# A two-layer streaming encoder step: the hand-over from the input projection to attention, norm and table factors in PSUM, and the places of eight output products

## What is computed

```python
# layer 0
h = rmsnorm(x, norm_mix[0])
q, k, v, u, g = split(h @ w_in)                     # u, g through gelu; 8 heads of 64
att = stick_breaking(q, k, v)                       # prompt: causal; sample: 512 cached rows + 64 new
sg  = u * (tril(w_s) @ g + b_s)                     # spatial gating in chunks of 128
x  += concat(att, sg) @ w_out
x  += swiglu(rmsnorm(x, norm_ffn[0]))               # hidden width 2816
# layer 1
h = rmsnorm(x, norm_mix[1])
s = scan(a * s + B h);  y = C s + d * h             # complex diagonal SSM, 64 groups of 64 states
x += glu(gelu(y) @ w_glu)
x += swiglu(rmsnorm(x, norm_ffn[1]))
y = rmsnorm(x, norm_final)
```

## Time and profile before

| | |
|---|---|
| median of 3 runs | 2650.52 us (2648.42 to 2651.08) |
| the profiled execution | 2645.23 us, its span 2643.1 us |
| busy share of the span | PE 95%, PEld 85%, DVE 46%, ACT 35%, POOL 50% |
| mean granted clock of PE | 0.972 of full speed |
| transfers | 322 MB, mean 122 GB/s |

### The profile page before, as it was taken

One profiled execution on the slowest core, in us unless ns is written; L12 is line 12 of the kernel. 1 busy time (PEld: TensorE's weight loads), 2 busy tenths in 40 slices (PEclk: granted clock), 3 DMA queues, 4 the chain that ended last, 5 costly groups with the idle time before them and its releaser, 6 DMA issues.

```text
span 2643.1 us, 39417 instructions
## 1 busy us (share of the span) xinstructions
PE 2506.9 (95%) x15914; PEld 2257.7 (85%) x15914; DVE 1221.8 (46%) x2074; ACT 926.2 (35%) x1334; POOL 1315.8 (50%) x840
## 2 busy tenths in 40 slices
PE   8999658899999989999999998999999999999998
PEld 6999646677778978899999987788887988999998
DVE  5896937765562242434343414544354133233233
ACT  5323237566552232312222323322224234221213
POOL 5465344655555554634343556544445556444444
PEclk9999879899999999999999999999999999999999
DMA  6227564334424555344444332445553222322221
GB/s 196 74 88 272 193 181 106 91 113 121 114 73 145 159 154 161 109 130 131 126 138 121 105 97 78 149 136 150 155 153 113 80 77 88 101 84 88 77 84 68
DMA packets 413731, 322.45 MB, mean 122 GB/s; under 512 B 86561, under 2 KB 370145, under 8 KB 412401
## 3 DMA queue, kind: packets, MB, share of 16 engines
q1 hardware_dynamic: 406464, 292.07, 37.5%
q0 software_dynamic: 5936, 26.69, 2.5%
q10 hardware_dynamic: 1152, 1.18, 0.1%
HBM read 258.78 MB, written 61.10 MB: 121 GB/s over the span
## 4 chain that ended last, share of the span: by engine, by line
PE 82%; DVE 8%; POOL 4%; DMA 3%; issue 2%; ACT 1%; SPq 0%; POOLq 0%; DVEq 0%; ACTq 0%
PE ps L256 24%; PE ps L257 23%; PE ps L258 23%; PE ps L752 3%; PE ps L764 2%; PE ps L1605 1%; PE ps L1601 1%; POOL wlo L250 1%; DMA mst<-mT 1%; DVE t L2071 1%; PE ps L744 1%; PE ps L740 1%; PE ps L1582 1%; DVE t L2073 1%; DVE nf L1351 1%
## 5 line engine op out<-in xcount | busy, mean ns | idle before, releaser
L250 POOL TENSOR_TENSOR wlo<-raw,whi 128x1024 fp32r<-128x1024 f32 x332 | 803.0, 2423 | 678.0 <-ACT whi L246 676.7
L256 PE MATMUL ps<-hB,whi 128*128 128x320 f32 (+1 forms) x1792 | 534.2, 298 | 3.4 <-POOL lB L1772 3.2
L246 ACT ACTIVATE whi<-raw 128x1024 fp32r<-128x1024 f32 x332 | 346.3, 1052 | 544.6 <-PE ps L258 403.7
L257 PE MATMUL ps<-lB,whi 128*128 128x320 f32 (+1 forms) x1792 | 531.2, 296 | 0.0
L258 PE MATMUL ps<-hB,wlo 128*128 128x320 f32 (+1 forms) x1792 | 531.2, 296 | 0.0
L1282 DVE TENSOR_TENSOR fb<-ps,ab 128x512 f32<-128x512 f32 (+2 forms) x156 | 83.5, 535 | 813.2 <-PE ps L258 722.9
L256 PE MATMUL ps<-rh,whi 128*128 128x512 f32 (+2 forms) x1056 | 356.5, 338 | 35.2 <-POOL rl L1252 21.9
L256 PE MATMUL ps<-hA,whi 128*128 128x512 f32 x896 | 358.3, 400 | 12.6 <-POOL lA L1240 12.3
L257 PE MATMUL ps<-lA,whi 128*128 128x512 f32 x896 | 351.7, 392 | 0.0
L258 PE MATMUL ps<-hA,wlo 128*128 128x512 f32 x896 | 351.4, 392 | 0.0
L257 PE MATMUL ps<-rl,whi 128*128 128x512 f32 (+2 forms) x1056 | 349.2, 331 | 0.0
(11 more groups left out here) (308 smaller groups left out, 3897.8 us busy)
## 6 DMA issues: line engine op xcount, KB each, us to landing
raw<-in_ffn_w_gate SPq DMA_DIRECT2D x88, 512.0 KB, 3.9
raw<-in_ffn_w_up SPq DMA_DIRECT2D x88, 512.0 KB, 3.8
raw<-in_ffn_w_down SPq DMA_DIRECT2D x88, 512.0 KB, 3.3
raw<-in_ssm_w_glu SPq DMA_DIRECT2D x32, 512.0 KB, 4.0
raw<-in_ab_w_in SPq DMA_DIRECT2D x20, 512.0 KB, 3.9
raw<-in_ab_w_out SPq DMA_DIRECT2D x16, 512.0 KB, 3.9
bt<-dBT SPq DMA_DIRECT2D x16, 512.0 KB, 5.1
tm<-dT SPq DMA_DIRECT2D x16, 512.0 KB, 4.2
```

The source lines that it names most:

```text
L246: act.activation(whi[:, slot(t), :], raw[:, t % 2, :], ACT.Copy).then_inc(sem("w_hi"), 1)
L250: pool.tensor_tensor(wlo[:, slot(t), :], raw[:, t % 2, :], whi[:, slot(t), :].bitcast(F32), ALU.subtract).then_inc(sem("w_lo"), 1)
L256: pe.matmul(out, wh, rh, start=first, stop=False)
L257: pe.matmul(out, wh, rl, start=False, stop=False)
```

## The change

Four parts: the SSM factors move to PSUM and their stores to earlier places; the loads of the hand-over are reordered and its conditions split in two; norm factors move to PSUM; six `outS` products go beside every second step.

```diff
-        g4, _ = plan(off_end + T * 4, ("g4", [P, 2, GP, 4], F32))
+        g4 = ps[:, 3, 256:512].rearrange("p (r j k) -> p r j k", r=2, k=4)
+        pbs = ps[:, 3, 0:2 * 8 * L].rearrange("p (r j k) -> p r j k", r=2, k=L)
+        pcs = ps[:, 3, 256:256 + 2 * 8 * (L + 1)].rearrange("p (r j k) -> p r j k", r=2, k=L + 1)
...
-        msum, mrm, oa = plan(off_w + 10 * D * 4, ("msum", [P, 2, 512], F32), ("mrm", [P, 2, 512], F32))
+        msum, mrm, oa = plan(off_w + 10 * D * 4, ("msum", [P, 2, 512], F32), ("mrm", [P, 512], F32))
+        ms3, oa = plan(off_w + 10 * D * 4 + 3 * 512 * 4, ("ms3", [P, 512], F32))
...
+        def products_done(eng):
+            eng.wait_ge(sem("acc_ready"), NC * IN_TILES)
+            eng.wait_ge(sem("z_lo"), 8)
+            eng.wait_ge(sem("mix_sent0"), 16 * 6)
+            eng.wait_ge(sem("mix_sent1"), 16 * 6)
...
-        new_slot([group("outS", 0, 0, m, [ts[m // 2]]) for m in range(4)])
-        for m in range(4, 8):
+        new_slot([group("outS", 0, 0, m, [ts[m // 2]]) for m in range(2)])
+        for m in range(2, 8):
+            new_slot(at=some_steps())
             new_slot([group("outS", 0, 0, m, [ts[m // 2]])], at=some_steps())
...
+        def mst_at(i):
+            return {2: nsq[:, 1, :], 3: ms3}.get(i, mst[:, i % 2, :])
         def mst_in(sp, i):
-            if i >= 2:
+            if i >= 4:
                 sp.wait_ge(sem("ms_lo"), i - 1)
+            if i == 2:
+                sp.wait_ge(sem("tables"), 18)
...
         def mid_sp(sp, ahead):
-            front_done(sp)
+            products_done(sp)
+            for i in range(4):
+                mst_in(sp, i)
+            sp.wait_ge(sem("tok_out0"), tok_sent(14))
             v_early(sp, 0)
             kq_early(sp, 1)
-            mst_in(sp, 0)
-            mst_in(sp, 1)
             x_load(sp, 0)
+            front_done(sp)
             v_early(sp, 1)
-            mst_in(sp, 2)
-            mst_in(sp, 3)
...
         def mid_act(act):
-            front_done(act)
+            products_done(act)
-            for S in SLOTS:
+            for no, S in enumerate(SLOTS):
+                if no == FIRST_DENSE:
+                    front_done(act)
...
         def mid_pe(pe):
-            pe.wait_ge(sem("kv_used"), kv_taken(len(TOKS)))
++                if no == FIRST_DENSE:
+                    pe.wait_ge(sem("kv_used"), kv_taken(len(TOKS)))
...
-                        if q >= 2:
-                            act.wait_ge(sem("m_f"), KD * (q - 1))
-                        act.activation(mrm[:, q % 2, 0:n], ps[:, G[g]["bank"], 0:n], ACT.Sqrt, bias=epsb[:, 0:1], scale=1.0 / D
+                        factor_free(act, q)
+                        act.activation(factor(q), ps[:, G[g]["bank"], 0:n], ACT.Sqrt, bias=epsb[:, 0:1], scale=1.0 / D
...
+        def factor(q):
+            k, half, c = NORMS[q]
+            n = HCH[half][c][1]
+            return mrm[:, 0:n] if q in (0, 2) else ps[:, 4 if c else 7, 0:n]
+        def factor_free(act, q):
+            if q == 1:
+                act.wait_ge(sem("o_out"), sum(v["last"] for v in units) - GROUPS_A)
+            elif q:
+                act.wait_ge(sem("m_f"), KD * (q if NORMS[q][2] == 0 else q - 1))
+            k, half, c = NORMS[q]
+            if k == 3 or q == 6:
+                act.wait_ge(sem("s_sh"), KD * (2 if k == 3 and half else 1))
...
-                p_ = [pb[:, r, j0:j0 + 8, :].unsqueeze(3).to_broadcast(sh) for r in range(2)]
+                own(dve.tensor_copy(pbs, pb[:, :, j0:j0 + 8, :]))
+                p_ = [pbs[:, r].unsqueeze(3).to_broadcast(sh) for r in range(2)]
...
-        PREP_AT = [12, 13, 14, 14, 15, 15, 16, 16, 17, 18, 19, 19]
+        PREP_AT = [(9, 0), (10, 0), (11, 0), (11, 1), (12, 1), (13, 0), (13, 1), (14, 0), (14, 1), (15, 0), (16, 0), (17, 0)]
...
+                if t == IN_TILES + 2:
+                    xg_free(sp)
+                    kq_first(sp)
                 if t - 4 in TOK_AT:
                     tok_store(sp, TOK_AT.index(t - 4))
-                if t == IN_TILES + 2:
-                    xg_free(sp)
-                    kq_first(sp)
```

More of the change, by code:

```diff
@@ L1028, in build @@
         NG = len(G)
+        FIRST_DENSE = G[0]["slot"]
         NSLAB = IN_TILES + len(SRC)
@@ L1097, in mst_in @@
                     sp.wait_ge(sem(f"o_stored{b}"), 16 * 4)
-            sp.dma_start(mst[:, i % 2, 0:n], mT[tile * P:(tile + 1) * P, s:s + n]).then_inc(sem(f"ms_in{i % 2}"), 16)
+            sp.dma_start(mst_at(i)[:, 0:n], mT[tile * P:(tile + 1) * P, s:s + n]).then_inc(sem(f"ms_in{i if i < 4 else i % 2}"), 16)
         def mst_cut(i):
@@ L1102, in mst_cut @@
             n = HALF[half][1]
-            return half, slice(tile * n, (tile + 1) * n), mst[:, i % 2, 0:n]
+            return half, slice(tile * n, (tile + 1) * n), mst_at(i)[:, 0:n]
         xs3 = xs.rearrange("p (f t) -> p f t", f=KD)
@@ L1166, in mid_act @@
                     half, cs, src = mst_cut(i)
-                    act.wait_ge(sem(f"ms_in{i % 2}"), 16 * (i // 2 + 1))
+                    act.wait_ge(sem(f"ms_in{i if i < 4 else i % 2}"), 16 if i < 4 else 16 * (i // 2))
                     if i == 4:
@@ L1231, in mid_pool @@
         def mid_pool(pool):
-            front_done(pool)
+            products_done(pool)
             pre_zero(pool)
-            for S in SLOTS:
+            for no, S in enumerate(SLOTS):
+                if no == FIRST_DENSE:
+                    front_done(pool)
                 for t in S["slabs"]:
@@ L1296, in mid_dve @@
         def mid_dve(dve):
-            front_done(dve)
-            for S in SLOTS:
+            products_done(dve)
+            for no, S in enumerate(SLOTS):
+                if no == FIRST_DENSE:
+                    front_done(dve)
                 gs, at = S["groups"], S["at"]
@@ L1331, in mid_dve @@
                         used(dve, rms_of[q])
-                        dve.reciprocal(mrm[:, q % 2, 0:n], mrm[:, q % 2, 0:n]).then_inc(sem("m_rr"), 1)
+                        dve.reciprocal(factor(q), factor(q)).then_inc(sem("m_rr"), 1)
                         dve.wait_ge(sem("m_rr"), q + 1)
-                    xf, rf = xh[half][:, cols_of(half, f, s, n)], mrm[:, q % 2, 0:n]
+                    xf, rf = xh[half][:, cols_of(half, f, s, n)], factor(q)
                     if q in SPLIT_NO:
@@ L2101, in prep_dve_block @@
                 sh = [P, 8, L + 1, 16]
-                p_ = [pc[:, r, j0:j0 + 8, :].unsqueeze(3).to_broadcast(sh) for r in range(2)]
+                own(dve.tensor_copy(pcs, pc[:, :, j0:j0 + 8, :]))
+                p_ = [pcs[:, r].unsqueeze(3).to_broadcast(sh) for r in range(2)]
                 c_ = [ct[:, r, j0:j0 + 8, :].unsqueeze(2).to_broadcast(sh) for r in range(2)]
@@ L2199, in store, with prep_stores @@
                 pool.dma_start(lo[j * P:(j + 1) * P, :], zlo[:].bitcast(F32)).then_inc(sem("z_stored"), 16)
+            def prep_stores(t, late):
+                for n in range(12):
+                    if PREP_AT[n] == (t, late):
+                        prep_pool_block(pool, n)
             for t in range(IN_TILES):
                 slab_lo(pool, t + 2)
-                for n in range(12):
-                    if PREP_AT[n] == t:
-                        prep_pool_block(pool, n)
+                prep_stores(t, 0)
                 if 2 <= t <= 8 and t % 2 == 0:
@@ L2214, in _ @@
                     cache_pool(pool, TOK_AT.index(t))
+                prep_stores(t, 1)
             at_pool_make(pool)
```

## The result

The changed kernel takes 2605.66 us (median of four runs, 2602.91 to 2605.96), the kernel before 2649.85 us: a ratio of 0.983, 95% interval 0.981 to 0.985, 44.2 us less.

The account below looks back on a forecast made before the run. TensorE's fixed-order queue was taken as the bound, time being won where it idles or its clock is low. Front 41, norms 10 and a slab split 1 made 52 us: 2650.5 - 52 = 2598 us, range 2584 to 2618.

Parts of the forecast that it names:

- Tables: VectorE's SSM tables: end at 297 us instead of 326; 20 us of waiting and 21 of holding go, 10 given back.
- My lower bound of 282 us: Earliest end forecast for VectorE's SSM tables, if no operation is held by GpSimd.
- GpSimd's queue: Earlier table stores ahead of GpSimd's weight-slab splits: cost 0, up to 10 us if VectorE is held as now.
- Hand-over: SyncE's loads before attention: 31.4 us query wait gone, mst issued at 311 to 315 us, first subtraction 45 us sooner.
- The rival of the crowding loads: Loads before attention land 12 to 18 us later, or products cost 2.8 us: 2610 to 2617 us; chance 0.19.
- Products beside units: Six output products beside attention units cost 1.0 us each, between 0 and 2.8; units take 72 us against 68.3.
- My bound of 45 - 17: Lower bound of the front's gain: first subtraction 45 us sooner, less 17 us.
- Front: Everything up to the seventeenth attention unit: gain 45 - 4 = 41 us.
- Norms: Norm factors in PSUM gain 10 us: 3 and 4 at the SSM's norms, 3 at the rl waits; ends 0 and 19.
- Square root, reciprocal and eight copies with PSUM: Square root and reciprocal in norms cost 0, or 9 us at worst; the tables' eight copies cost 2.4 us.
- The slower rival: Table products with a broadcast PSUM operand cost more; at 3.2 us each the kernel takes 2697 us; chance 0.04.
- Each sign that I had named: Query wait under 3 us, products near 1.22, mst before 316, first subtraction at 328 to 338, seventeenth 65 to 76 later.

Follow-up runs that it names:

- e1: Changed kernel with the table factors back in SBUF and without the eight copies; 2624.8 us (0.990 to the kernel before).
- e6: Changed kernel with the 2 MB of xA coming in four loads of 512 KB; 2600.9 us (0.982 to the kernel before).
- e10: e7 with the norm factors back in SBUF; 2605.4 us (0.984 to the kernel before).
- e7: Changed kernel with xA in four loads and the second half's first SSM product behind its slot's gate product; 2593.6 us (0.979 to the kernel before).
- e11: Kernel before, with only the second half's first SSM product moved behind its slot's gate product; 2649.3 us (1.000).
- e2: Changed kernel with the norm factors back in two buffers of SBUF; 2610.4 us (0.985 to the kernel before).
- e8: Changed kernel with the twelve table stores back at tiles 12 to 19, at the end of the tile; 2635.4 us (0.994 to the kernel before).
- e12: Changed kernel with the twelve table stores at the very places of before, behind the tile's slab split; 2630.0 us (0.993 to the kernel before).
- e9: e7 with four spatial products ahead of the first unit and four beside units 0 to 3; 2591.3 us (0.979 to the kernel before).
- e3: Changed kernel with four spatial products ahead of the first unit and four beside units 0 to 3; 2603.5 us (0.983 to the kernel before).
- e4: Changed kernel with the hand-over of before (whole-front wait, two spatial buffers, first key loads behind stores); 2610.7 us (0.985 to the kernel before).

## Why the prediction was right, and where its sizes were off

The direction and the range held: 2598 us forecast, 2605.7 measured, 52 us of gain forecast against 44.2 (38.9 on the spans). By its steps:

- **Tables, end forecast at 297 us: 285.9.** The mechanism was right, the term mis-sized. I took 21 us of holding from the four groups that I had before me; summed over all 48 products it was 26 us. And I gave back 10 us for holding that would move to the subtractions; but subtractions and copies were held before already, and that only grew from about 14 to 16 us. My lower bound of 282 us doesn't follow from the terms that I gave, which make 287 without the 10 given back; the 26 us make 282. The error did no harm: keys issued at 291.5 land before TensorE asks at 308.
- **GpSimd's queue, costed at 0.** Right, with the factors in PSUM, and the wait for a slab's split that the sum took 1 us for (1.4 us, ahead of 293.56 us) is gone. My bound of up to 10 us without them was too low: e1 shows 15 us of starving.
- **Hand-over.** First `mst` before 316 us: 310.4. First subtraction at 333 us: 331.06. `xA` landing at 329 to 332 us and the first eviction waiting for it: 329.85. The rival of the crowding loads is this same fact, and e6 prices it at 4.8 us, but it was inside the forecast's times.
- **Products beside units, 1.0 us each: mis-sized.** The 16 units took 74.7 us instead of 72. Against 63.2 us without products the six cost 11.5 us, slab splits included, where I had 9; two beside four units cost 2.2 us each, more than the 1.3 of four beside four and not less, as I had argued. That a product costs less when it is spread did not hold. (My bound of 45 - 17 set six whole products against 68.3 us, which holds four already; by the row of 15.8 us and the splits it is 45 - 15.)
- **Front, 41 us: 41.1** at the seventeenth unit. The mis-sizings cancel: the first unit came 47.4 us sooner instead of 45, and the units lost 6.3 us instead of 4. That it fits to 0.1 us is luck, since two executions of one code lie up to 4 us apart here. Of the gain 3.3 us are gone again ahead of the `hp` norm: at the first sum of squares and at the evictions into `xA` near 942 us TensorE stands as long as before (2.88 and 2.05 us), but the spell at the lower clock falls otherwise (below). I had no term for that, and it is none of the change's: it differs as much between executions of one code.
- **Norms, 10 us: this is the step that failed**, and only in part. The two parts that stand free came in: 3 us for the first half's `hp`, measured 2.8; of the 3 us at the `rl` waits some 2 stayed (1.4 by the end of norm 4's stage, 0.7 at the second half's, 2139 us). The 4 us for the second half's `hp` came in as evictions (4.3 us of waiting became 0.4) and were lost some 10 us further on, to the exchange through DRAM, where TensorE now waits 5.9 us instead of 0.6. (The prediction read two waits, 6.3 us, as that norm's; one of them, 2.05 us near 980 us, near 942 in the changed kernel, stands elsewhere, and it stayed.) I named the stall that goes and not what is late next. That the factors in PSUM are worth the forecast's 10 us when TensorE has other work ahead of that exchange is what e10 against e7 shows: 11.8 us.
- **Square root, reciprocal and eight copies with PSUM:** no cost seen; the copies took 0.30 and 0.31 us each. A product took 1.214 us with a PSUM factor (L2111) against 1.216 us with two SBUF operands not held (L2114 in e1). The fixed cost that the Trainium skill, "VectorE: DVE Perf Modes", section on the TRN2 errata, gives a PSUM source on top of an SBUF source's does not show in these two figures.
- **The slower rival** is refuted by the product groups alone: no broadcast product in PSUM took over 1.36 us.

Each sign that I had named held: the query wait, the products' times, the first `mst`, the first and the seventeenth subtraction, the evictions' waits under 3 us. The sum was off all the same, since none of the signs looked behind the second half's norm, where the exchange stands and, at the very end, the 2 us without a known cause.

By undoing, the parts are worth: factors of the tables 19 us, tiles of the stores 24, hand-over 5, norm factors 5 (12 with the product behind the exchange moved), order of the products nothing. They don't sum to 44, because the two table edits need one another. What the old tables, both parts undone, would cost under the new hand-over was not tried.

## What to carry to other kernels

When a stall is removed from an engine, follow the data it makes to their next user before booking the gain: here a store and reload through DRAM (10 us behind a slow norm, 12 to 14 behind a fast one) was hidden by the slow norm and appeared when the norm was fast. Two edits on a chain that two engines walk in turn have to be tried together; alone each showed less than half of the end that both gave. And moving work to another place in a full engine's list has to be priced in both places: what two products won by leaving the head of the list, 5.9 us, they cost again beside the units, 5.4 us. Before reading a small step between two traces, look for a second execution of the same code: here they differed by up to 4 us in the front.

## What was not expected of the hardware

A copy with one operand is held too: L2127, 64 elements, takes 2.42 to 2.44 us in three of four instances and 0.20 us in the fourth, while a product with one operand in PSUM beside it never is. The same section of the Trainium skill, "SBUF — State Buffer", lists copies among the operations that can enter a 2-port mode and so contend with GpSimd, which fits; whether this copy ran in such a mode no run shows.

TensorE's clock answered otherwise to the same stall. Behind the first sum of squares TensorE stands 2.88 us in every trace; in the stretch that follows, the granted clock is 0.60 in the changed kernel (us, busy by engine, PEclk, DMA share, GB/s),

```profile
460.00:464.00 4.00, 2.68 (x7) 1.68 (x7) 0.00 (x0) 2.66 (x3) 3.47 (x2) 0.60 0.00 0
```

and full in the kernel before, where it falls some 2 us later against the stall:

```profile
501.00:504.00 3.00, 1.62 (x9) 1.18 (x10) 0.12 (x1) 2.61 (x3) 3.00 (x2) 1.00 0.00 0
```

It is not the change that does this. In e11, which up to there is the kernel before, the same stretch behind the same stall has 0.78:

```profile
503.70:506.70 3.00, 1.62 (x3) 0.69 (x4) 0.00 (x0) 2.12 (x2) 3.00 (x2) 0.78 0.00 0
```

From the seventeenth unit to norm 0 e11 loses 1.5 us against the trace of before; the changed kernel, e2 to e8 and e12 lose 1.6 to 1.8 us there, e9 1.0, e10 nothing, and e1 gains 1.9. Near 942 us it is the same: e3 and e4, which have the changed kernel's code there, lose nothing where the changed kernel loses 1.5. Why the fall comes sooner in one execution than in another stays open.
